# Scales of the first norm as columns, squares summed on GpSimd, x and ctx in one tile

## What is computed

```python
mx = (jax.nn.silu(c) @ ada_w[layer] + ada_b[layer]).reshape(b, 1, N_MOD, D_MODEL)
mc = (jax.nn.silu(c_ctx) @ ada_w[layer] + ada_b[layer]).reshape(N_MOD, D_MODEL)
hx = modulate(rmsnorm(x, norm1_g[layer]), mx[:, :, 0], mx[:, :, 1])
hc = modulate(rmsnorm(ctx, norm1_g[layer]), mc[0], mc[1])
ux = hx @ w_in[layer]
uc = hc @ w_in[layer]
```

## Time and profile before

| what | value |
|---|---|
| median of 3 runs | 879.65 us |
| the profiled execution | 880.59 us |
| its span | 878.8 us |
| TensorE busy | 852.7 us (97%) |
| VectorE, ScalarE, GpSimd busy | 579.3, 461.7, 436.9 us |
| HBM read | 158.85 MB, 182 GB/s over the span |

### The profile page before, as it was taken

The page is one execution under the profiler, slowest core; times in us unless marked ns, Lnnn a source line. Parts: engine busy times, 40 slices in busy tenths (PEclk is TensorE's granted clock), DMA queues, the critical chain, the costliest instruction groups (busy, mean ns, idle before and its releaser), DMA issues.

```text
span 878.8 us, 16212 instructions
## 1 busy us (share of the span) xinstructions
PE 852.7 (97%) x6572; PEld 813.2 (93%) x6572; DVE 579.3 (66%) x1184; ACT 461.7 (53%) x753; POOL 436.9 (50%) x215
## 2 busy tenths in 40 slices
PE   6799999999999999999999999999999999999996
PEld 2288999999799999999999999999999999999996
DVE  6978987975667697676767779586447433333425
ACT  5442244443656565555555864555446555555545
POOL 0856422223562588888888300200000788878781
PEclk9899999999999999999999999999999999999998
DMA  9958575654477466666566546254435466565651
GB/s 342 358 175 275 161 256 172 207 186 154 145 226 228 121 188 198 189 178 187 183 184 184 158 152 191 90 192 128 161 108 182 144 192 192 171 195 178 186 158 49
DMA packets 45759, 160.96 MB, mean 183 GB/s; under 512 B 5218, under 2 KB 5490, under 8 KB 45556
## 3 DMA queue, kind: packets, MB, share of 16 engines
q1 hardware_dynamic: 45680, 159.91, 57.5%
q10 hardware_dynamic: 4, 0.01, 0.0%
HBM read 158.85 MB, written 1.05 MB: 182 GB/s over the span
## 4 chain that ended last, share of the span: by engine, by line
PE 90%; DVE 3%; ACT 2%; DMA 2%; POOL 1%; issue 1%; SPq 0%; DVEq 0%; POOLq 0%; ACTq 0%
PE bank L630 19%; PE bank L634 19%; PE bank L632 19%; PE bank L958 4%; PE bank L956 4%; PE bank L960 4%; PE bank L696 3%; PE bank L700 3%; PE bank L698 3%; PE bank L761 2%; PE bank L845 2%; POOL wlo L497 1%; PE bank L721 1%; DMA ctxT<-in_ctxT 1%; PE bank L1086 1%
## 5 line engine op out<-in xcount | busy, mean ns | idle before, releaser
L497 POOL TENSOR_TENSOR wlo<-raw,whi 128x1024 fp32r<-128x1024 f32 (+1 forms) x175 | 406.9, 2344 | 385.5 <-ACT whi L1166 385.4
L1166 ACT ACTIVATE whi<-raw 128x1024 fp32r<-128x1024 f32 (+1 forms) x253 | 258.6, 1027 | 83.2 <-PE bank L634 57.1
L630 PE MATMUL bank<-h2h,whi 128*128 128x256 f32 x872 | 248.3, 285 | 0.0
L634 PE MATMUL bank<-h2l,whi 128*128 128x256 f32 x872 | 247.0, 283 | 0.7 <-DVE h2l L1579 0.7
L632 PE MATMUL bank<-h2h,wlo 128*128 128x256 f32 x872 | 246.8, 283 | 0.0
L1579 DVE SCALAR_TENSOR_TENSOR accs<-bank,vec,accs 128x189 f32<-128x189 f32 (+4 forms) x440 | 161.2, 433 | 72.2 <-ACT accs L1441 72.2
L634 PEld LDWEIGHTS bank<-h2l,whi 128*128 128x128 f32 x872 | 167.3, 192 | 1.3 <-DVE h2l L1579 1.3
L630 PEld LDWEIGHTS bank<-h2h,whi 128*128 128x128 f32 x872 | 167.3, 192 | 0.7 <-issue 0.3
L632 PEld LDWEIGHTS bank<-h2h,wlo 128*128 128x128 f32 x872 | 167.3, 192 | 0.1
L497 DVE TENSOR_TENSOR wlo<-raw,whi 128x1024 fp32r<-128x1024 f32 x78 | 94.4, 1221 | 23.7 <-ACT whi L1166 23.2
L956 PE MATMUL bank<-gh,whi 128*128 128x256 f32 x320 | 90.6, 283 | 0.0
(11 more groups left out here) (322 smaller groups left out, 1666.9 us busy)
## 6 DMA issues: line engine op xcount, KB each, us to landing
raw<-in_up SPq DMA_DIRECT2D x88, 512.0 KB, 3.6
raw<-in_w_in SPq DMA_DIRECT2D x45, 512.0 KB, 3.9
raw<-in_down SPq DMA_DIRECT2D x44, 512.0 KB, 4.0
ada_kT<-in_adaT SPq DMA_DIRECT2D x22, 512.0 KB, 4.3
raw<-in_w_out SPq DMA_DIRECT2D x16, 512.0 KB, 4.4
raw<-in_w_in_t SPq DMA_DIRECT2D x12, 512.0 KB, 4.5
ada_vM<-in_adaT SPq DMA_DIRECT2D x10, 512.0 KB, 4.5
ada_buf<-in_adaT SPq DMA_DIRECT2D x8, 512.0 KB, 10.7
```

The source lines that it names most:

```text
L497: return e.tensor_tensor(wlo[:, j % HL, 0:k], raw[:, j % RAW, 0:k], whi[:, j % HL, 0:k].bitcast(F32), ALU.subtract)
L630: e.matmul(ps, wh[:, k, :], xh(k), start=k == 0, stop=False)
L634: t = e.matmul(ps, wh[:, k, :], xl(k), start=False, stop=k == KTILES[name] - 1)
L1166: e.activation(whi[:, j % HL, 0:(k1 - k0) * 128], raw[:, j % RAW, 0:(k1 - k0) * 128], ACT.Copy).then_inc(S.hi.up(j))
```

## The change

- The scales are computed as columns: for each slab, eight matmuls with a 128x128 block of ada_sc as weights and the two columns of cs moving, into 16 columns of one PSUM bank. The rows, their copies (arow) and the transposes go. `rows`' last two events become one, `scale`.
- TensorE takes the mean of the squares before k = 3 and spreads the roots before k = 4; it no longer does them before k = 0 and k = 1. VectorE takes the inverse after j = 3, not after j = 0.
- GpSimd adds the squares, VectorE does not.
- x and ctx become two halves of one tile xc. ScalarE squares both in one instruction, GpSimd multiplies both in one. ctx now lies where ada_kT lies, so SP waits for the last product xr before it issues adaT 16 to 18.
- ScalarE copies cb after the fourth square. VectorE's pairs of row sums begin with the row of c, whose copy is waited for first, and no longer start with that of c_ctx.
- The first two columns of the projection are computed in parts: tiles 0 to 2 of both, then 3 to 7 of both.

```diff
--- before.py
+++ after.py
@@ -252,7 +252,8 @@
         put("amul", 11.5, [128, 8, 2])
         put("lbs", 11.625, [128, 20])
         put("sm", 11.75, [128, 32])
-        put("xT", 12, [128, 8, L])
+        put("xc", 12, [128, 2, 8, L])
+        M["xT"], M["ctxT"] = M["xc"][:, 0, :, :], M["xc"][:, 1, :, :]
         put("kT", 20, [128, 8, L])
         put("vM", 28, [128, 2, 1024])
         put("raw", 36, [128, RAW, 1024])
@@ -266,13 +267,11 @@
         put("ada_buf", Z + 48, [128, 6, 1024])
         put("ada_sc", Z + 76, [128, 8, 1024])
         put("junk", Z + 32, [128, 1024])
-        put("arow", Z + 108, [2, 1024])
         put("hr", Z + 32, [128, 2, 512])
         put("xg", Z, [128, 8, L])
         put("hch", Z, [128, 8, 512], F32R)
         put("hcl", Z + 16, [128, 8, 512], F32R)
         put("memT", Z + 36, [128, 8, L])
-        put("ctxT", Z + 40, [128, 8, L])
         put("f", Z + 32, [128, 2, 2, 4, L])
         put("A", Z + 40, [128, 2, 4, L])
         put("kk", Z + 48, [128, 2, 2, 4, L])
@@ -363,7 +362,7 @@
             chunk = signal("chunk", range(NCH))
             summed = signal("summed", [(f, j) for f in range(2) for j in (1, 3, 5)])
             total = signal("total", ("x", "h0", "h1", "w_out", "mem", "down", "g0", "g1", "w_out2", "wo", "down2"))
-            rows = signal("rows", ("cb", "cbx", "rows", "turned"))
+            rows = signal("rows", ("cb", "cbx", "scale"))
             keyT = signal("keyT", range(4))
             state = signal("state", range(2))
             score = signal("score", SCAN)
@@ -376,7 +375,7 @@
             att = signal("att", ATT)
 
             hi = signal("hi", range(NCH))
-            rowc = signal("rowc", ("crow", "cs", "cb", "arow0", "arow1"))
+            rowc = signal("rowc", ("crow", "cs", "cb"))
             sqx = signal("sqx", range(8))
             lbe = signal("lbe")
             root = signal("root", NORMS)
@@ -561,7 +560,7 @@
 
         def row_of(who):
 
-            first = 4 if who else 2
+            first = 4 if who else 0
             return psum[:, first:first + 2, :].rearrange("p a b -> p (a b)")
 
 
@@ -737,10 +736,6 @@
 
 
             one_row = cst[0:1, 1:2].broadcast_to((1, 128))
-            rows = []
-            for h in range(2):
-                slot, _ = lin_ring.take(("rows", h), S.rowc, f"arow{h}")
-                rows.append(banks[slot])
             for who, ring, first in ((0, lin_ring, 0), (1, aux_ring, 4)):
                 w.wait_ge(S.const, "cst")
                 w.wait_ge(S.rowc, "crow")
@@ -751,22 +746,18 @@
                 t.then_inc(S.rows.up(("cb", "cbx")[who]))
 
             w.wait_ge(S.rowc, "cs")
-            means("x", M["sqs"][:, 0, :], 4, S.ssx, 7, (S.by_row, "x"))
+            slot, _ = aux_ring.take("scale", S.mod, "amul")
             for k in range(KT):
-                if k == 1:
+                if k == 3:
+                    means("x", M["sqs"][:, 0, :], 4, S.ssx, 7, (S.by_row, "x"))
+                if k == 4:
                     w.wait_ge(S.ident, 0)
                     spread("x", aux_bank("x"))
                 w.wait_ge(S.sc[k], 0)
-                for h in range(2):
-                    t = e.matmul(rows[h][0:2, :], M["cs"][:, k, :], M["ada_sc"][:, k, h * 512:h * 512 + 512],
-                                 start=k == 0, stop=k == KT - 1)
-            t.then_inc(S.rows.up("rows"))
-            slot, _ = aux_ring.take("turned", S.mod, "amul")
-            w.wait_ge(S.rowc, "arow1")
-            for j in range(8):
-                t = e.transpose(banks[4 + slot][:, 2 * j:2 * j + 2], M["arow"][:, j * 128:j * 128 + 128],
-                                ident[0:2, 0:2])
-            t.then_inc(S.rows.up("turned"))
+                for j in range(8):
+                    t = e.matmul(banks[4 + slot][:, 2 * j:2 * j + 2], M["ada_sc"][:, k, j * 128:j * 128 + 128],
+                                 M["cs"][:, k, :], start=k == 0 and j == 0, stop=k == KT - 1, skip_group_check=True)
+            t.then_inc(S.rows.up("scale"))
             for k in range(KT):
                 ht_bank_free[k] = aux_ring.take(("ht", k), S.hcl, k)[1]
 
@@ -774,7 +765,7 @@
             for j in range(2):
                 slot, free = lin_ring.take(("ff", j), S.sgf, j)
                 columns.append(("w_in", IN_FF + j, banks[slot][:, :], free))
-            lins(columns, hc_all)
+            lin_parts(columns, hc_all, 3)
             for j in range(2, 8):
                 slot, free = lin_ring.take(("ff", j), S.sgf, j)
                 lin("w_in", IN_FF + j, banks[slot][:, :], hc_all, free)
@@ -1233,11 +1224,12 @@
             e.activation(cs[:, :, 1], col("c_ctx", 0, 8), ACT.Silu).then_inc(S.rowc.up("cs"))
             for i in range(8):
                 w.wait_ge(S.x[i // 4], 0)
-                e.activation(M["sqs"][:, i, 0:L], xT[:, i, :], ACT.Square)
                 w.wait_ge(S.ctx[i // 4], 0)
-                e.activation(M["sqs"][:, i, L:2 * L], M["ctxT"][:, i, :], ACT.Square).then_inc(S.sqx.up(i))
-            w.wait_ge(S.rows, "cb")
-            e.activation(M["cb"][:, :], row_of(0), ACT.Copy).then_inc(S.rowc.up("cb"))
+                e.activation(M["sqs"][:, i, :].rearrange("p (v t) -> p v t", v=2), M["xc"][:, :, i, :],
+                             ACT.Square).then_inc(S.sqx.up(i))
+                if i == 3:
+                    w.wait_ge(S.rows, "cb")
+                    e.activation(M["cb"][:, :], row_of(0), ACT.Copy).then_inc(S.rowc.up("cb"))
             w.wait_ge(S.const, "cst")
             sqrt_next()
             w.wait_ge(S.total, "x")
@@ -1245,10 +1237,6 @@
             by_row("x", M["rsx"][:, :], aux_bank("x"))
             w.wait_ge(S.lb, "less")
             e.activation(lbs[:, 4:12], lbs[:, 4:12], ACT.Exp).then_inc(S.lbe.up(0))
-            w.wait_ge(S.rows, "rows")
-            for h in range(2):
-                e.activation(M["arow"][:, h * 512:h * 512 + 512], lin_bank(("rows", h))[0:2, :],
-                             ACT.Copy).then_inc(S.rowc.up(f"arow{h}"))
             splits(2)
             for k in range(KT):
                 w.wait_ge(S.scaled, k)
@@ -1632,25 +1620,17 @@
             tt(lbs[:, 4:8], a0, lbs[:, 0:4], ALU.subtract)
             tt(lbs[:, 8:12], a1, lbs[:, 0:4], ALU.subtract).then_inc(S.lb.up("less"))
 
-            ssx = M["sqs"][:, 0, :]
-            for i in range(1, 8):
-                w.wait_ge(S.sqx, i)
-                if i > 1:
-                    w.wait_ge(S.ssx, i - 1)
-                tt(ssx, ssx, M["sqs"][:, i, :], ALU.add).then_inc(S.ssx.up(i))
             two = (128, 8, 2)
             for j in range(KT):
+                w.wait_ge(S.rowc, "cb")
+                ada_sum(j, 0, junk[:, :], row_of(0)).then_inc(own())
                 w.wait_ge(S.rows, "cbx")
-                w.wait_ge(S.rowc, "cb")
-                if j:
-                    w.wait_ge(own_dve, own_dve.n)
-                ada_sum(j, 1, junk[:, :], row_of(1)).then_inc(own())
                 w.wait_ge(own_dve, own_dve.n)
-                ada_sum(j, 0, None, row_of(0)).then_inc(S.ada.up(j))
-                if j == 0:
+                ada_sum(j, 1, None, row_of(1)).then_inc(S.ada.up(j))
+                if j == 3:
                     inverse("x")
-            w.wait_ge(S.rows, "turned")
-            turned = aux_bank("turned")[:, 0:16].rearrange("p (j w) -> p j w", w=2)
+            w.wait_ge(S.rows, "scale")
+            turned = aux_bank("scale")[:, 0:16].rearrange("p (j w) -> p j w", w=2)
             tt(turned, turned, col("ada_b", 8, 8).unsqueeze(2).broadcast_to(two), ALU.add).then_inc(own())
             w.wait_ge(own_dve, own_dve.n)
             stt(amul[:, :, :], turned, 1.0, col("norm1_g", 0, 8).unsqueeze(2).broadcast_to(two), ALU.add,
@@ -2182,12 +2162,16 @@
                         low_half(e, j).then_inc(S.lo_pool.up(j))
                     at[0] = j + 1
 
+            ssx = M["sqs"][:, 0, :]
+            for i in range(1, 8):
+                w.wait_ge(S.sqx, i)
+                if i > 1:
+                    w.wait_ge(S.ssx, i - 1)
+                e.tensor_tensor(ssx, ssx, M["sqs"][:, i, :], ALU.add).then_inc(S.ssx.up(i))
             w.wait_ge(S.by_row, "x")
             for k in range(KT):
-                for v, src in enumerate((xT, M["ctxT"])):
-                    t = e.tensor_tensor(M["xr"][:, k, v * L:v * L + L], src[:, k, :], M["rsx"][:, v * L:v * L + L],
-                                        ALU.mult)
-                t.then_inc(S.xr.up(k))
+                e.tensor_tensor(M["xr"][:, k, :].rearrange("p (v t) -> p v t", v=2), M["xc"][:, :, k, :],
+                                M["rsx"][:, :].rearrange("p (v t) -> p v t", v=2), ALU.mult).then_inc(S.xr.up(k))
             los(ch("w_in", IN_FF + 4) + HL)
             w.wait_ge(S.msk, 0)
             e.tensor_copy(M["mask"][:, :], M["maskf"][:, :]).then_inc(S.mask.up(0))
@@ -2258,10 +2242,11 @@
                 ada(j)
                 scale(j)
             loads(RAW)
+            w.wait_ge(S.xr, KT - 1)
```

(2 more changed lines are left out.)

## The result

The changed kernel takes **888.12 us** (median of 4 runs, 887.42 to 888.62), the kernel before 880.03 us beside it (4 runs, 878.97 to 880.68). The ratio is 1.0093, with a 95% interval from 1.0081 to 1.0105: 8.1 us slower. The forecast was 889.7 us, by the case of the slow clock.

The account below looks back on a forecast made before the run. TensorE, busy 97%, bounds the kernel; the change lies in its first 50 us. Slow scale columns +10.1 us, other terms 0, on 880.59 give 890.7, for the median 889.7 us; own range 887 to 892, with rivals 877 to 892.

Parts of the forecast that it names:

- the case of the slow clock: Scale columns: stream stays at 1.2 GHz, amul at 45.6 against 35.52 us, +10.1 us; chance 0.55.
- What would show it: Signs: records 0.22 us apart, no DMA wait on slabs 1 to 7, amul at 45 to 46 us, VectorE waiting.
- held at the inverse: VectorE's row shifts: stands from 21.8 us, root and reciprocal at 25.95, ends at 36.1; costs nothing.
- The pitch: Scale columns on TensorE: 0.222 us a record at the slow level.
- One price for a load, or two: Weight loads: skill's 107 ns whatever the clock gives 13.7 us for 128; rows differ, so measurement decides.
- GpSimd's sum: Adding the squares on GpSimd: done at 17.9 us, TensorE asks at 23.6, so hidden.
- The floor: Transfers of ada_sc: slab 7 there at 30.8 us, old path needing 2.5 us of matmuls behind it.
- wait for the last product: SP's wait before ada 16 to 18: they land by 46 us, wanted after 60; costs nothing.
- term of 0: First two projection columns in parts: same 15.4 us as before, bounds -4.5 to +6.4 us.
- The range's lower half: Range 877 to 892 us takes in the neutral case and about half the faster one, besides both slower cases.
- the clock rising with the stream: Rival on the scale columns: clock rises and holds, -2.3 us, 877.4 us; chance 0.22.

Follow-up runs that it names:

- warmed run: Changed kernel with six unused dense 512-column f32 matmuls ahead of slab 0 only; 891.86 us in a single execution.

## Why the prediction was right, and where its terms were off

*The case was right.* Records at 0.213 us throughout, no wait for slabs 1 to 7, VectorE held at the inverse for 3.4 us (some 4): as listed under "What would show it", except that amul is there at 44.06 instead of 45 to 46. The warmed run shows the mechanism behind it, the same records at half the pitch while the clock was up. The case had been given 0.55.

*The pitch was mis-sized.* The prediction took 0.2225 us a record from the eight loads of L713, a row whose duration includes the end of its last record. In a long stream it is 0.2134: 128 x 0.0091 = 1.2 us. Means and spread, 1.70 and 1.84 us from start to start instead of 1.78 and 2.0, and the start at 12.78 give another 0.35. That is the whole 1.54 us between 45.6 and 44.06. What is left of the forecast's error is 0.5 us that the kernel made up behind amul (8.5 us late there, 8.0 in the span), against 0.4 us by which the median of the kernel before stands higher with its fourth run (880.03, not 879.65).

*One price for a load, or two.* The columns took twice as long at the one level as at the other, 0.213 against 0.108 us. The Trainium skill ("TensorE: Matmul & The Clock Gate", section "LDWEIGHTS (loading the stationary operand)") has one price, the number of columns divided by 1.2 in ns, which works out to 107 ns for 128. By the warmed stretch of that run the trace agrees at the fast level alone; at the slow one, which ruled here, the measurement decides, as the prediction chose.

*GpSimd's sum* ended at 18.24 us (forecast 17.9) and was asked for at 23.0; the products took 9.87 us (9.8).

*The floor.* The prediction had the old path bound by the last landing, estimated at 30.8 us, with 2.5 us of matmuls behind it. The rows of the kernel before show no wait for a slab; the run with rows and true transposes shows one, at 30.84 us, 1.9 us of matmuls behind it. The forecast did not hang on this, since it compares amul with the 35.52 us that were read.

*VectorE* waited at the inverse from 21.8 to 25.2, with the reciprocal done at 25.4 (25.95), and was through with the row sums at 35.4 (36.1), 8.2 us before it was wanted. *SP's* wait for the last product ended at 40.80. The kernel with rows and true transposes has all of these, and is no slower than before: hidden, as forecast.

*The first two columns* took 15.18 us, from 45.93 to 61.11, with a term of 0 on 15.37. Right in size, in part by luck. The prediction said that the clock has to come back first, as before, and it did: the pitch halved 7.7 us behind the first matmul, 7.9 in the kernel before. But the cause was another. Before, the wait for wlo stood among the first matmuls; after, that wait was gone because the scales came late and both low halves lay ready at 45.4 us, and the parts held TensorE back behind VectorE instead. Without the parts the clock was back after 3.1 us and the two columns took 12.45. So the parts cost 2.5 us that the text did not price; it noted the pace of 1.49 us a tile and left it. What the wait had cost went, what the parts cost came, and the term of 0 is the difference.

*The range's lower half* rested on the clock rising with the stream. The runs give that case no support: the clock rose in none of the long column streams. The prediction's evidence against it, twelve records of L1148 with the clock at 0.50 behind them, pointed the right way.

## What to carry to other kernels

A long stream of weights that are loaded for one or two moving columns is priced at TensorE's slow level, unless a trace shows such a stream at the fast one (here sixteen such records behind dense work ran 0.12 us apart, and in the warmed run about forty ran 0.108 apart before the clock fell): a reshaping that saves instructions elsewhere can turn a stage at or near the floor of its transfers into one that weight loads bound. Letting the large operand move past narrow weights for all that lies beside the transfers, with the turned form for the last slab only, brought the scales about 1 us sooner here. Work in parts likely pays where an operand is late (1.1 us here), and costs where all lie ready and another engine sets the pace of the tiles (2.5 us here).

## What was not expected of the hardware

- The granted clock fell from 1.00 to 0.50 with TensorE busy for the whole of both windows around it (the warmed run, 25 to 27 us).
- The eight turns of a 2x128 block take 0.65 us as transposes (8 records) and 1.94 us as f32 matmuls (16 records), both with the granted clock at 1.00.
- In the profiles where TensorE waits for slab 0 of ada_sc it came between 12.61 and 14.25 us, with the same issues ahead of it, and in the run with rows slab 7 came 1.2 us later than in the one with true transposes. Single profiles therefore differ by as much as the steps of about 1 us that are weighed here; those rest on medians.
